# Indexer stage: head-sum stores ahead of the large prefetch loads, the prompt's scores stored from ScalarE

## The reference

```
s = jnp.einsum('bqhe,ble->bqhl', qib, ki).astype(jnp.float32) * (D_IDX ** -0.5)
score = jnp.einsum('bqhl,bqh->bql', jax.nn.relu(s), wib.astype(jnp.float32)) * (H_IDX ** -0.5)
score = jnp.where((kpos[None, :] <= pb[:, None])[None], score, -jnp.inf)
_, idx = lax.top_k(score, top)
```

## Time and profile before

| | us |
|---|---|
| median of 3 runs | 2198.08 (2195.49 to 2212.44) |
| profiled execution, device time | 2195.09 |
| its span, first to last instruction | 2193.2 |
| end of phase `idx`, from the span's start (first DMA issue of `sb`) | 278.83 |

### The profile page before, as it was taken

The page is one execution under the profiler, slowest core; times in us unless marked ns, Lnnn a source line. Parts: engine busy times, 40 slices in busy tenths (PEclk is TensorE's granted clock), DMA queues, the critical chain, the costliest instruction groups (busy, mean ns, idle before and its releaser), DMA issues. The chain is left out here.

```text
span 2193.2 us, 40283 instructions
## 1 busy us (share of the span) xinstructions
PE 1966.9 (90%) x15288; PEld 1623.0 (74%) x15288; DVE 1222.0 (56%) x2538; ACT 888.9 (41%) x1508; POOL 150.8 (7%) x445
## 2 busy tenths in 40 slices
PE   6996678679989999999899689899997899999997
PEld 5995256446669999976599566677775799999665
DVE  5224488798565555544631478645544655555445
ACT  2220355347424444433221278634442244444332
POOL 3001200100001111100000000001100011111000
PEclk9997889889999999999989689999999999999998
DMA  5447799654226666432233664134303266664322
GB/s 156 136 152 262 191 343 362 208 183 152 78 66 206 219 207 209 158 122 80 67 110 87 187 198 104 54 138 174 156 29 116 66 215 211 209 207 163 117 80 72
DMA packets 170271, 342.84 MB, mean 156 GB/s; under 512 B 38494, under 2 KB 107150, under 8 KB 166138
## 3 DMA queue, kind: packets, MB, share of 16 engines
q1 hardware_dynamic: 154942, 201.78, 29.2%
q10 hardware_dynamic: 11228, 84.20, 11.3%
q0 software_dynamic: 3968, 55.06, 6.4%
HBM read 313.44 MB, written 98.40 MB: 188 GB/s over the span
## 5 line engine op out<-in xcount | busy, mean ns | idle before, releaser
L235 PE MATMUL ffn_acc<-x_h,ffn_wh 128*128 128x288 f32 x1408 | 303.0, 297 | 6.8 <-DVE ffn_wl L227 6.8
L235 PE MATMUL ffn_acc<-x_l,ffn_wh 128*128 128x288 f32 x1408 | 302.7, 297 | 0.0
L235 PE MATMUL ffn_acc<-x_h,ffn_wl 128*128 128x288 f32 x1408 | 302.4, 297 | 0.0
L235 PEld LDWEIGHTS ffn_acc<-x_h,ffn_wh 128*128 128x128 f32 x1408 | 227.9, 190 | 7.6 <-issue 7.5
L235 PEld LDWEIGHTS ffn_acc<-x_l,ffn_wh 128*128 128x128 f32 x1408 | 227.9, 190 | 0.0
L235 PEld LDWEIGHTS ffn_acc<-x_h,ffn_wl 128*128 128x128 f32 x1408 | 227.9, 190 | 0.0
L227 DVE TENSOR_TENSOR ffn_wl<-ring,ffn_wh 128x1024 fp32r<-128x1024 f32 (+2 forms) x94 | 154.9, 1653 | 73.6 <-ACT ffn_wh L2267 71.2
L2208 PE MATMUL ffn_acc<-ffn_wh,x_h 128*128 128x512 f32 x352 | 143.2, 407 | 7.8 <-DVE ffn_wl L227 7.8
L2293 ACT COPY ffn_ext<-ffn_acc 128x288 f32<-128x288 f32 x88 | 35.2, 400 | 271.2 <-PE ffn_acc L235 260.4
L2210 PE MATMUL ffn_acc<-ffn_wh,x_l 128*128 128x512 f32 x352 | 139.6, 397 | 0.0
L2209 PE MATMUL ffn_acc<-ffn_wl,x_h 128*128 128x512 f32 x352 | 139.1, 395 | 0.0
(11 more groups left out here) (454 smaller groups left out, 4062.0 us busy)
## 6 DMA issues: line engine op xcount, KB each, us to landing
out_s_b_kv<-state_b_kv ACTq DMA_DIRECT2D x80, 768.0 KB, 8.0
ring<-ffn_up SPq DMA_DIRECT2D x44, 1024.0 KB, 10.6
ring<-ffn_down SPq DMA_DIRECT2D x44, 512.0 KB, 3.3
sb_k<-state_b_kv SPq DMA_DIRECT2D x8, 2048.0 KB, 11.3
sb_v<-state_b_kv SPq DMA_DIRECT2D x8, 2048.0 KB
proj_ab_w<-w_in_ab SPq DMA_DIRECT2D x11, 1024.0 KB, 5.9
ring<-w_in_c SPq DMA_DIRECT2D x7, 1024.0 KB, 5.4
hT_ab<-proj_ab_stage ACTq DMA_DIRECT2D x22, 288.0 KB, 2.5
```

The source lines that it names most:

```text
L235: done = pe.matmul(o, weights, x, start=start, stop=stop)
```

## The change

SP's list in `idx` gets a new order, and three stores change the issuing engine. In each stage SP now waits for the copied head sums and issues their store first; the keys' prefetch of stage 1 follows behind that store, and ahead of the row loads of stage 1. The values' prefetch moves to the end of SP's list, behind the last row loads. The three stores of the prompt's scores leave SP; ScalarE issues them near the end of its list, between the ReLU of the half 14 and that of the half 15 (halves count from 0).

```
             for u in range(NB // 2):
+                sp.wait_ge(part_done, u + 1)
+                sp.dma_start(parts[u], part[:, :]).then_inc(parts_stored, 16)
                 if u == 1:
                     ahead.load_keys(sp)
-                if u == 3:
-                    ahead.load_values(sp)
-                    for i in range(1, NQ):
-                        L = (i + 1) * P
-                        sp.wait_ge(p_summed, len(steps) + i)
-                        sp.dma_start(pscore[:, i - 1, 0:L], p_score[:, i - 1, 0:L]).then_inc(p_stored, 16)
-                sp.wait_ge(part_done, u + 1)
-                sp.dma_start(parts[u], part[:, :]).then_inc(parts_stored, 16)
                 sp.wait_ge(parts_stored, 16 * (u + 1))
                 load_rows(sp, u, 0)
                 if u + 1 < NB // 2:
                     load_rows(sp, u, 1)
+            ahead.load_values(sp)
             sp.wait_ge(p_stored, 16 * (NQ - 1))
             sp.wait_ge(keep.pending, keep.pending_count)
...
                 if n == PAIRS:
                     act.wait_ge(new_dots, 1)
                     act.activation(relu_new[:, :, :], dots_new.rearrange("p (b t) -> p b t", b=NB), ACT.Relu, scale=IDX_SCALE).then_inc(new_relu, 1)
+                if n == PAIRS + 3:
+                    for i in range(1, NQ):
+                        L = (i + 1) * P
+                        act.wait_ge(p_summed, len(steps) + i)
+                        act.dma_start(pscore[:, i - 1, 0:L], p_score[:, i - 1, 0:L]).then_inc(p_stored, 16)
             act.wait_ge(parts_stored, 16 * (NB // 2))
             load_rows(act, NB // 2 - 1, 1)
```

## The result

| | before | with the change |
|---|---|---|
| median of 15 runs each, us | 2199.16 (2190.99 to 2212.44) | 2181.80 (2172.93 to 2195.69) |
| ratio, 95% interval | | 0.9939 (0.9921 to 0.9958) |
| profiled execution: device time, us | 2195.09 | 2189.65 |
| its span, us | 2193.2 | 2187.8 |

A forecast was written before the change was run, and what follows sets the result against it. The end of idx was taken to hang on stores and row loads through SP's queue. Gains 1.5 + 2.9 + 7.2 = 11.6 us took 2195.09 to 2183.5; with 3.0 for the median, 2187 us, range 2180 to 2196.

The forecast's parts named there:

- VectorE's stall: In idx, the 5.86 us wait before the copy of stage 2's head sums goes; the gain there only 1.5 us.
- stage 3's store: At the end of idx, with nothing large ahead, it lands in 2.05 instead of 9.26 us, gaining 7.2.
- SP's issue time: In idx, issuing values and prompt stores ahead of stage 3's store, 2.92 us, goes.
- Stage 1's store in 2.05 us: In idx, issued ahead of the keys, it lands in 2.05 us like stage 2's, by about 241.9.
- Stage 2's store at 258.1: In idx, behind the keys and stage 1's rows, it lands at 258.1 instead of 259.61, gaining 1.5 us.
- the keys' 17.5 us: In idx, the keys take 17.5 us as before, starting 3.3 us later, so they end at 257.3.
- rival 4: In idx, bias table loads are done, keys need less, stage 2's store lands at 255; gain 14.7, 2183.5; chance 0.09.
- The prompt's stores on ScalarE at nothing: Late in idx, 1.1 to 1.8 us of issue delays half 15's ReLU, hidden while stage 2's store lands at 258.1.
- bound of 2.0 us: In idx, 576 KB of prompt stores taking the keys' place in the transfers delay stage 2's store to 260.1.
- Values ahead of the keys of sequence 1 at nothing: At the start of sb, keys land about 278, wanted at 278.1; cost 0 to 2.4 us, taken as 0.
- rival 1: In sb, the load stream stays behind compute because 2.6 MB of values moved in; 2.4 us, 2189.5; chance 0.15.
- Rivals 2, 3 and 5: idx: second store sticks, 2190.5, 0.10; queue order fails, 2193, 0.06; slower or no gain, second store very late, 2200.5, 0.05.

The follow-up runs named there:

- e1: Against the kernel before, only stage 1's store goes ahead of the keys; values and prompt scores stay ahead of stage 3's store on SP; ratio 0.9970.
- e2: Against the kernel before, only the values' prefetch moves to the end of SP's list; ratio 0.9953.
- e9: The change, with GpSimd issuing the bias table's 16 loads earlier, behind its third gather instead of its last; ratio to the kernel before 0.9936.
- e6: The change, with GpSimd holding the bias table's 16 loads until stage 2's head sums are copied; ratio to the kernel before 0.9946.
- e8: The change, with the prompt's stores on SP again, behind the last row loads and ahead of the values; ratio to the kernel before 0.9963.
- e3: Against the kernel before, only the prompt's stores move to ScalarE, SP keeping the rest of its order; ratio 0.9996.
- e4: The change, with the values of sequence 0 loaded in sb behind the keys of sequence 1; ratio to the kernel before 0.9933.
- e5: The change, with keys ahead of stage 0's store and values behind stage 1's store; ratio to the kernel before 0.9919.
- e7: The change, with keys ahead of stage 0's store, values behind stage 1's, and the bias table's loads early too; ratio to the kernel before 0.9940.
- r2: Repeat of the change with keys ahead of stage 0's store and values behind stage 1's; ratio to the kernel before 0.9920.

## Why the prediction was right, and where it was not

The total was right, 11.6 us forecast, 13.4 (9.2 to 17.4) measured, but in part by luck: stage 2's store landed 3.2 us earlier than forecast, sb lost 2.6 us that the sum had put at nothing, and the two errors nearly cancel. In the two profiles they leave 14.8 - 2.6 = 12.2 us.

- *VectorE's stall, stage 3's store, SP's issue time*: as forecast. The last store's 2.05 us is the figure of the forecast, and e1 and e2 show the two parts separately.
- *Stage 1's store in 2.05 us*: not so, it landed 4.9 us after its issue (first row: KB, us to landing). The bias table's loads ran beside it; with these out of the way it took 2.3 us in e9 (second row) and 2.4 in e6. Nothing came of it, since VectorE wanted the tile 253.29 - 244.08 = 9.2 us after the issue.

```profile
idx_parts<-idx_part SPq DMA_DIRECT2D x1, 256.0 KB, 4.9
```

```profile
idx_parts<-idx_part SPq DMA_DIRECT2D x1, 256.0 KB, 2.3
```

- *Stage 2's store at 258.1* is the step that failed, by its size. That is 29.2 us after the first store; it landed 26.1 after it. The term that was wrong is the keys' 17.5 us, "kept whole" from a start 3.3 us later: they took 246.65 + 11.4 - 244.47 = 13.6 us and came in no later at all, at 24.6 instead of the 28.4 of the forecast (257.3 - 228.88). The 0.8 us from the last key to the landing of the store were 1.5 (26.1 - 24.6). That the table makes the difference is what e6, e9 and the stretches show. It is what I had given rival 4 as its mechanism (the table's loads done by then), and its price, 14.7 us, is the 14.8 that idx gained.
- *The prompt's stores on ScalarE at nothing*: right, but the cover is thin. The last head sums ended at 258.10 + 1.05 = 259.15, the store they were hidden behind landed at 259.55. The three issues took ScalarE 1.33 us:

```profile
256.02 1.33 ACTq L1083 DMA_DIRECT2D pscore<-idx_p_score  x3
```

  The bound of 2.0 us, by which these transfers would hold back stage 2's store, did not show: 26.1, 26.1 and 26.6 with them on ScalarE, 26.4 (e1) and 26.5 (e8) without. The Trainium skill ("DMA: Bandwidth & Descriptors", Issuing engines are not separate DMA queues) expects only the issue time to be saved; e3, with 2.4 us of idx for 1.76 us of issue, comes near to that, and the 2.0 us that I had worked out beside it were not lost.
- *Values ahead of the keys of sequence 1 at nothing*: wrong, the second step that failed. The keys landed 14.2 us after the phase's start (269.12 + 13.8 - 268.67), wanted at 10.9; rival 1 came with 2.87 us of waiting, beyond the 2 us that I had named as a sign of being wrong. The loss in sb is 1.0 to 2.9 us in the executions with the values in the stream, 2.6 in the change's first; the bound was 2.4. Of these 2.6, 1.0 is there by sequence 1, where e4 shows that the order is the cause (its subtraction 25.81 us after the phase's start before, 26.80 with the change, 25.52 in e4); 1.4 more come by sequence 4 (65.42 before, 67.80 with the change), from the gap that goes with the late transfer of instructions. So rival 1's reason covers part of its price.
- Rivals 2, 3 and 5 did not come: stage 2's store was early, the last rows took 3.0 us as before (267.35 - 264.34), nothing got slower.

## What to carry to other kernels

A small store that is waited for belongs ahead of a large prefetch in the same queue; look then for the next store behind that prefetch, for it inherits the wait. A prefetch that is taken out of one phase stands ahead of the next phase's first load: ask which of the two is wanted first. Before a prefetch is moved for time, see what else the DMA engines carry in the stretch that it loses and in the one that it gains.

## What the runs showed of the hardware that was not expected

Sixteen loads of 32 KB from GpSimd's queue raised the share of the DMA engines from 28% to 70% and the rate only from 78 to 125 GB/s (e9 and change, 2 to 11 us after the first store); a store of 256 KB beside them took 4.9 us instead of 2.3, and the keys beside them ended at the same time whether issued at 5.9 or 11.0 us. 576 KB of stores right ahead of a small store in the same queue cost it 0.35 us (2.40 against 2.05, e2), 2.5 MB of loads 6.8 us (276.66 - 267.83 = 8.83, e3). A gap of TensorE of 1.1 to 1.2 us, with nothing in the profile to wait for, went, in all five executions that have it, with a transfer of 16 KB of instructions that began some 4 us later than in the nine without the gap. And identical work ahead of the change ended up to 5.9 us apart in different executions (first store at 228.25 to 234.13; e5, e7, e9 and r2, which move work ahead of it, left out), so that a few us can be read only between events of one execution.
